# Adding the bias rows one tile per expert, and grouping small matmuls by columns, in a GLA/attention/MoE block

## The reference

```python
h = layer_norm(x, ln_in_g, ln_in_b)
...
cum_f = jnp.cumsum(jax.nn.log_sigmoid(f_logit), axis=1)       # forget sums, 512 tokens x 8 heads
...
h = layer_norm(DEEPNORM_ALPHA * h + mixed @ w_out, ln_mix_g, ln_mix_b)
logits = h @ w_router + b_router                              # (512, 32)
top_val, top_idx = lax.top_k(logits, 4)
gates = jax.nn.softmax(top_val, axis=-1)
for e in range(32):                                           # rows of the tokens that chose e
    gu = x_e @ w_gate_up[e] + b_gate_up[e]
    glu = min(gu[:, :1024], 7) * sigmoid(1.702 * ...)
    y_e = ((clip(gu[:, 1024:]) + 1) * glu) @ w_down[e] + b_down[e]
out = layer_norm(DEEPNORM_ALPHA * h + sum over e of gate * y_e, ln_ffn_g, ln_ffn_b)
```

## Time and profile before

| what | value |
|---|---|
| median of 3 runs | 1829.23 us (1829.06 to 1830.15) |
| the profiled execution | 1828.79 us |
| its span, first to last instruction | 1827.1 us |
| PE busy | 1759.0 us, 96% |
| DVE busy | 1360.6 us, 74% |
| ACT busy | 1094.7 us, 60% |
| POOL busy | 294.0 us, 16% |
| mean granted PE clock | 0.984 |

### The profile page before, as it was taken

How to read it: one execution, slowest core, us unless ns; L and a number is a source line. 1 busy time by engine, 2 the same in 40 slices (tenths; PEclk the granted TensorE clock), 3 DMA queues, 4 the chain that set the end, 5 groups by cost and what they waited for, 6 DMA issues and landing times.

```text
span 1827.1 us, 23598 instructions
## 1 busy us (share of the span) xinstructions
PE 1759.0 (96%) x8353; PEld 1434.7 (79%) x8354; DVE 1360.6 (74%) x1180; ACT 1094.7 (60%) x875; POOL 294.0 (16%) x222
## 2 busy tenths in 40 slices
PE   6999999999999999989999999999999999999993
PEld 5787788888887877767888888888888888888872
DVE  6324533442436789869999999999999999999995
ACT  3433223454423267757777777877777777787772
POOL 3000000000000054141212212121221221212211
PEclk9999999999999999999999999999999999999996
DMA  7322122212233399999999999999999999999973
GB/s 255 102 82 70 54 85 70 70 47 93 81 103 139 138 319 363 369 337 360 368 373 388 366 363 388 369 371 387 372 372 383 383 366 371 391 366 366 391 294 109
DMA packets 115448, 487.42 MB, mean 267 GB/s; under 512 B 18822, under 2 KB 49542, under 8 KB 66250
## 3 DMA queue, kind: packets, MB, share of 16 engines
q1 hardware_dynamic: 99474, 455.66, 64.9%
q0 software_dynamic: 15920, 31.12, 6.1%
q10 hardware_dynamic: 8, 0.01, 0.0%
HBM read 476.12 MB, written 27.84 MB: 276 GB/s over the span
## 4 chain that ended last, share of the span: by engine, by line
PE 90%; DVE 4%; DMA 3%; issue 1%; ACT 1%; POOL 0%; ACTq 0%; DVEq 0%; POOLq 0%
PE psA L1560 21%; PE psA L1562 21%; PE psA L1561 21%; PE psX L1562 6%; PE psX L1561 6%; PE psX L1560 6%; PE psX L1567 3%; DMA acc_dram<-y_t,didx 1%; DMA acc_dram<-h,ridx 1%; PE psX L1731 1%; PE psX L1717 1%; PE psX L1690 1%; PE psA L1922 1%; DVE orstd L1165 1%; PE psX L1740 0%
## 5 line engine op out<-in xcount | busy, mean ns | idle before, releaser
L1325 DVE TENSOR_TENSOR wlo<-raw,whi 128x2048 fp32r<-128x2048 f32 x382 | 863.4, 2288 | 64.7 <-ACT whi L925 63.6
L925 ACT CAST whi<-raw 128x2048 fp32r<-128x2048 f32 x382 | 724.5, 1913 | 199.5 <-PE psA L1562 173.0
L1560 PE MATMUL psA<-whi,xT_hi 128*128 128x512 f32 x1020 | 401.1, 393 | 0.9 <-issue 0.9
L1562 PE MATMUL psA<-whi,xT_lo 128*128 128x512 f32 x1020 | 397.7, 390 | 0.0
L1561 PE MATMUL psA<-wlo,xT_hi 128*128 128x512 f32 x1020 | 397.6, 390 | 0.0
L1560 PEld LDWEIGHTS psA<-whi,xT_hi 128*128 128x128 f32 x1020 | 192.0, 188 | 41.3 <-issue 2.5
L1562 PEld LDWEIGHTS psA<-whi,xT_lo 128*128 128x128 f32 x1020 | 191.8, 188 | 40.1
L1561 PEld LDWEIGHTS psA<-wlo,xT_hi 128*128 128x128 f32 x1020 | 192.0, 188 | 38.5
L1560 PE MATMUL psX<-whi,aT_hi 128*128 128x512 f32 x512 | 204.3, 399 | 14.1 <-DVE wlo L1325 7.7
L1561 PE MATMUL psX<-wlo,aT_hi 128*128 128x512 f32 x512 | 201.5, 393 | 0.0
L1562 PE MATMUL psX<-whi,aT_lo 128*128 128x512 f32 x512 | 201.4, 393 | 0.0
(11 more groups left out here) (350 smaller groups left out, 2059.6 us busy)
## 6 DMA issues: line engine op xcount, KB each, us to landing
raw<-in_w_gate_up SPq DMA_DIRECT2D x254, 1024.0 KB
raw<-in_w_down SPq DMA_DIRECT2D x128, 1024.0 KB
raw<-in_w_in SPq DMA_DIRECT2D x32, 1024.0 KB
raw<-in_w_gla_proj SPq DMA_DIRECT2D x4, 1024.0 KB
raw<-in_w_fox_proj SPq DMA_DIRECT2D x4, 1024.0 KB
raw<-in_w_out SPq DMA_DIRECT2D x4, 1024.0 KB
xt<-in_x SPq DMA_DIRECT2D x4, 512.0 KB, 6.1
h_dram<-xt POOLq DMA_DIRECT2D x4, 512.0 KB, 5.1
```

Source lines behind the costliest of these rows:

```text
L925: s_.copy(xsplit(c)[0], xraw(slot)).then_inc(hi_ready, 1)
L1325: v.tensor_tensor(lo, xraw(slot), hi.bitcast(F32), ALU.subtract).then_inc(lo_ready, 1)
L1560: mm(dst, sh, mh, start=first, stop=False)
L1562: return mm(dst, sl, mh, start=False, stop=last)
```

## The change

- **Bias rows.** `add_bias` now takes a tile t and an expert i. `body(3)` to `body(6)` each issue one of the four additions, behind the gather, and wait for its landing before the scatter. Ahead of it stands a wait that the scatter before has landed. Experts 1 to 6 are written out and the loop starts at 7.
- **Drain.** GpSimd executes a drain between the loop and the last expert.
- **Forget sums.** In L1709 the loop over `r` becomes the innermost: successive products go to PSUM partitions 0 to 7 and 32 to 39 in turn.
- **Router.** The eight products of a tile no longer add up in one 32-partition strip: product k goes to strip k mod 4, two per strip. ACT copies all 128 partitions of the bank, and a product with `ident4` (four 32 x 32 identities on top of each other), which is an ordinary matmul and no transpose, turns and sums the four strips. GpSimd makes `ident4` with a memset and four affine selects, each waiting for the one before, ahead of its wait for `h_out`.
- **Counts.** DVE keeps `msum`, the sum of the earlier tiles' `member`, in `choose(2)` and `choose(3)`; `positions` takes at most two products.

The diff:

```diff
--- before.py
+++ after.py
@@ -188,7 +188,7 @@
     lprod = at("lprod", 172 + 2, [P, TOPK, E])
     lpos = at("lpos", 191.75, [P, TOPK])
     weight = at("weight", 176.5, [P, TT, E])
-    logitsT = at("logitsT", 179, [E, P])
+    logitsT = at("logitsT", 179, [P, P])
     logits = at("logits", 179.5, [P, TT, E])
     gate_s = at("gate_s", 187, [P, TT])
     gate_r = at("gate_r", 187.125, [P, TT])
@@ -236,6 +236,8 @@
     ones_r = at("ones_r", 200.75, [P, P], F32R)
     b_rt = at("b_rt", 201.25, [P, E])
     fl = at("fl", 201.375, [P, TT, FH])
+    ident4 = at("ident4", 201.5, [P, E])
+    msum = at("msum", 201.625, [P, E])
     small = at("small", 201.75, [P, 256])
     sel = at("sel", 203, [P, FH * P], F32R)
 
@@ -593,6 +595,11 @@
         pool.wait_ge(small_lo, 2)
         for s, part in enumerate((bias_hi, bias_lo)):
             g.dma_start(bgu_dram[s].rearrange("(p c) -> p c", p=P), part[:]).then_inc(bias_out, 16)
+        g.memset(ident4[:], 0.0).then_inc(blank_ready, 1)
+        for r in range(4):
+            pool.wait_ge(blank_ready, r + 1)
+            g.affine_select(out=ident4[:], in_=ident4[:], pattern=[[-1, E]], compare_op=ALU.not_equal, fill=1.0,
+                            base=-E * r, channel_multiplier=1).then_inc(blank_ready, 1)
 
         pool.wait_ge(h_out, 16 * TT)
         pool.wait_ge(half_done, 2 * NCD)
@@ -608,7 +615,7 @@
         g.memset(ltab[:, :, 1], 0.0).then_inc(blank_ready, 1)
         g.iota(lval[:, :, :, 0], [[P, TT], [0, TOPK]], base=0, channel_multiplier=1,
                allow_small_or_imprecise_dtypes=True).then_inc(blank_ready, 1)
-        pool.wait_ge(blank_ready, 3)
+        pool.wait_ge(blank_ready, 8)
         g.dma_start(list_dram.rearrange("(p e) c -> p e c", p=P), ltab[:]).then_inc(list_blank, 16)
         for t in range(TT):
             pool.wait_ge(h2_norm, 2 * (t + 1))
@@ -674,30 +681,29 @@
         g.dma_start(lnffn_g[:], bcast(a["ln_ffn_g"][0])).then_inc(lnffn_in, 16)
         g.dma_start(lnffn_b[:], bcast(a["ln_ffn_b"][0])).then_inc(lnffn_in, 16)
 
-        def add_bias():
-
-            pool.wait_ge(y_out, 16 * 2)
+        def add_bias(t, i):
+
             pool.wait_ge(ridx_ready, 1)
-            for t in range(TT):
-                pool.wait_ge(stage_ready, TT + t + 1)
-                g.indirect_dma_start(acc_dram, bass.IndirectOffsetOnAxis(ap=ridx[:, t:t + 1], axis=0), h2[:, t, :], None,
-                                     bounds_check=token_bound, oob_is_err=False,
-                                     compute_op=ALU.add).then_inc(bias_added, 16)
-            pool.wait_ge(bias_added, 16 * TT)
+            pool.wait_ge(stage_ready, TT + t + 1)
+            pool.wait_ge(y_out, 16 * (i - 1))
+            g.indirect_dma_start(acc_dram, bass.IndirectOffsetOnAxis(ap=ridx[:, t:t + 1], axis=0), h2[:, t, :], None,
+                                 bounds_check=token_bound, oob_is_err=False, compute_op=ALU.add).then_inc(bias_added, 16)
+            pool.wait_ge(bias_added, 16 * (t + 1))
 
         def body(i, last):
             if not last:
                 pool.wait_ge(gu_done, i + 1)
                 load_bgu(i + 1)
                 gather(i + 3, i + 2)
-            if isinstance(i, int) and i == 3:
-                add_bias()
+            if isinstance(i, int) and 3 <= i < 3 + TT:
+                add_bias(i - 3, i)
             scatter(i - 1)
 
-        for i in range(1, 4):
+        for i in range(1, 3 + TT):
             body(i, False)
-        with pool.Fori(4, E - 1) as i:
+        with pool.Fori(3 + TT, E - 1) as i:
             body(i, False)
+        pool.drain()
         body(E - 1, True)
 
         pool.wait_ge(tab_ready, E + 3)
@@ -945,7 +951,7 @@
             act.wait_ge(lg_done, t + 1)
             if t >= 1:
                 act.wait_ge(lg_turned, t)
-            s_.copy(logitsT[:], psX[0:E, 0, 0:P]).then_inc(lg_out, 1)
+            s_.copy(logitsT[:], psX[:, 0, 0:P]).then_inc(lg_out, 1)
 
         def gate_exp(t):
             act.wait_ge(ge_in, t + 1)
@@ -1282,6 +1288,9 @@
             seq.link(v.tensor_tensor(logits[:, t, :], logits_at(t), b_rt[:], ALU.add))
             seq.link(v.max(top_v[:, t, :], logits[:, t, :]))
             seq.link(v.max_index(top_i[:, t, :], top_v[:, t, :], logits[:, t, :]))
+            if t >= 2:
+                before = member[:, 0, :] if t == 2 else msum[:]
+                seq.mark(v.tensor_tensor(msum[:], before, member[:, t - 1, :], ALU.add))
             seq.link(v.tensor_copy(top_f[:, t, :], top_i[:, t, :]))
             seq.link(v.tensor_tensor(hot[:, t], iota[:, 0:E].unsqueeze(1).broadcast_to(shape),
                                      top_f[:, t, 0:TOPK].unsqueeze(2).broadcast_to(shape), ALU.is_equal))
@@ -1702,10 +1711,10 @@
                     for u in range(t + 1):
                         tri = incl if u == t else ones
                         mm(psX[:, 0, t * FH:(t + 1) * FH], tri[:], lsf[:, u, :], start=u == 0, stop=u == t)
-                for r in range(2):
-                    for t in range(TT):
-                        for u in range(t + 1):
-                            tri = incl if u == t else ones
+                for t in range(TT):
+                    for u in range(t + 1):
+                        tri = incl if u == t else ones
+                        for r in range(2):
                             ins = mm(psX[32 * r:32 * r + FH, 1, t * P:(t + 1) * P], lsf[:, u, :], tri[:],
                                      start=u == 0, stop=u == t)
                 ins.then_inc(f_done, 1)
@@ -1771,10 +1780,12 @@
         def route(t):
             if t >= 1:
                 pe.wait_ge(lg_out, t)
-            for k in range(KT):
-                if k % 4 == 0:
-                    pe.wait_ge(h2T_evac, 2 * t + k // 4 + 1)
-                ins = mm(psX[0:E, 0, 0:P], w_rt[:, k, :], h2T[:, k, t * P:(t + 1) * P], start=k == 0, stop=k == KT - 1)
+            for half in range(2):
+                pe.wait_ge(h2T_evac, 2 * t + half + 1)
+                for r in range(4):
+                    k = 4 * half + r
+                    ins = mm(psX[E * r:E * (r + 1), 0, 0:P], w_rt[:, k, :], h2T[:, k, t * P:(t + 1) * P],
+                             start=half == 0, stop=half == 1)
             ins.then_inc(lg_done, 1)
 
         def turn_logits(t):
@@ -1785,14 +1796,16 @@
                 pe.wait_ge(mem_ready, t)
             if 1 <= t < TT - 1:
                 pe.wait_ge(placed, t)
-            nc.tensor.transpose(logits_at(t), logitsT[:], ident[0:E, 0:E]).then_inc(lg_turned, 1)
+            if t == 0:
+                pe.wait_ge(blank_ready, 5)
+            mm(logits_at(t), logitsT[:], ident4[:], start=True, stop=True).then_inc(lg_turned, 1)
 
         def positions(t):
             pe.wait_ge(mem_ready, t + 1)
-            for u in range(t + 1):
-                tri = strict if u == t else ones
-                ins = mm(psX[:, 1, P + t * E:P + (t + 1) * E], tri[:], member[:, u, :], start=u == 0, stop=u == t)
-            ins.then_inc(pos_done, 1)
+            dst = psX[:, 1, P + t * E:P + (t + 1) * E]
+            if t >= 1:
+                mm(dst, ones[:], member[:, 0, :] if t == 1 else msum[:], start=True, stop=False)
+            mm(dst, strict[:], member[:, t, :], start=t == 0, stop=True).then_inc(pos_done, 1)
 
         def pick(t):
             pe.wait_ge(placed, t + 1)
```

## The result

| | before | after |
|---|---|---|
| median of 4 runs each | 1829.14 us (1828.49 to 1830.15) | 1809.77 us (1808.28 to 1810.97) |
| ratio | | 0.9893, 95% interval 0.9876 to 0.991 |
| profiled execution, its span | 1827.1 us | 1809.4 us |
| mean granted PE clock | 0.984 | 0.988 |

A forecast was written before the change was run, and what follows sets the result against it. PE, busy 1759.0 of 1827.1 us, was taken to bound the kernel. Gains of 11.4 (bias rows), 1.8 (forget sums), 2.9 (router and counts) and 0 (drain) summed to 16.1 us: forecast 1813.1 us, range 1810.5 to 1818.5.

## What to carry to other kernels

Price what happens behind the last product as a stage of its own: read how long each queue's closing drain runs past the landing of the last DMA, and if it does, put a drain where its engine idles anyway, late in the program. When work is taken off an engine that another one limits, its idle time may cost it its clock, so look whether cheap work fills the gap. A block of extra DMA traffic beside a saturated weight stream should be spread until the lead has regrown between two parts, not merely to one part per stage.

## What was not expected of the hardware

- A drain on GpSimd took 17.24 us in the loop's shadow and made the closing one 3.65 instead of 11.36 us; the closing drain ran 0.17, 0.83, 2.99 and 8.2 us past the last landing behind 3, 19, 63 and 127 or more GpSimd DMAs since the drain before.
- Four column strips of float32 products ran 16 records in 0.57 us, against 1.86 on one strip, 3.3 times as fast.
- Behind the same idle time of 1.97 or 1.98 us the granted clock fell to 1.2 GHz in seven profiles and stayed at 2.4 in one.
